# A decoder block with retention, gated DeltaNet and PEER experts on one core: norms held as columns, a search list of 112 sums, and another dealing of the expert turns

## The reference, cut to what matters

```python
h = rmsnorm(x, ln1_w); proj = h @ w_in        # 14 blocks of 256 columns, and 8 columns a, b
# retention, 4 heads (q, k of 64, v of 128), chunks of 128 tokens
# gated DeltaNet, 4 heads of 128: q, k, v = silu(causal conv of 4 taps)
q_g = q_g * rsqrt(sum(q_g * q_g) + eps)        # per token and head
k_g = k_g * rsqrt(sum(k_g * k_g) + eps)
# kkt = (beta k) k^T * lmask, triangular solve, o = S^T q / sqrt(128), S updated per chunk
x = x + concat(y_r, y_g) @ w_out
h2 = rmsnorm(x, ln2_w)
q = (h2 @ wq)                                  # 8 heads x 2 halves x 128
s = q . sub_keys                               # 128 scores per head and half
s1, i1 = top_k(s[first half], 16); s2, i2 = top_k(s[second half], 16)
cand = s1[:, None] + s2[None, :]               # 256 sums per head
best, pos = top_k(cand, 16)                    # 16 experts per head, 128 per token
gate = softmax(best)
x = x + sum_k gate_k * gelu(u[id_k] . h2) * v[id_k]
y = rmsnorm(x, lnf_w)
```

## Time and profile before

| | |
|---|---|
| median of 3 runs | 3363.88 us (3355.34 to 3367.5) |
| the profiled execution | 3368.8 us, its span 3367.0 us |
| mean granted TensorE clock | 0.858 |
| busy: PE, DVE, ACT, POOL | 2454.9, 2158.9, 1171.7, 1177.1 us |
| bytes moved by DMA | 1266.28 MB, mean 376 GB/s |
| gathers (queue 0), weights and others (queue 1) | 1073.81 MB, 183.84 MB |

### The profile page before, as it was taken

How to read it: one execution, slowest core, us unless ns; L and a number is a source line. 1 busy time by engine, 2 the same in 40 slices (tenths; PEclk the granted TensorE clock), 3 DMA queues, 4 the chain that set the end, 5 groups by cost and what they waited for, 6 DMA issues and landing times.

```text
span 3367.0 us, 35982 instructions
## 1 busy us (share of the span) xinstructions
PE 2454.9 (73%) x12432; PEld 1395.4 (41%) x12432; DVE 2158.9 (64%) x5332; ACT 1171.7 (35%) x3379; POOL 1177.1 (35%) x1030
## 2 busy tenths in 40 slices
PE   7579878646889968755879968855788757865555
PEld 6478445313457534411456624611355324521111
DVE  0525684788556785588746677487846677477444
ACT  1121533334432543234324343335233253333222
POOL 0002342433433334343423334343433324344442
PEclk9788999877899988867999979977889879987777
DMA  6047999998999999998999989999899989999998
GB/s 243 12 163 282 415 368 392 387 421 360 400 415 395 421 369 405 382 421 361 406 419 382 421 367 393 400 421 414 360 409 420 422 367 411 419 394 422 422 421 344
DMA packets 176438, 1266.28 MB, mean 376 GB/s; under 512 B 20096, under 2 KB 20096, under 8 KB 23808
## 3 DMA queue, kind: packets, MB, share of 16 engines
q0 software_dynamic: 147456, 1073.81, 77.8%
q1 hardware_dynamic: 26928, 183.84, 13.6%
q10 hardware_dynamic: 1872, 6.33, 0.5%
HBM read 1259.71 MB, written 4.19 MB: 375 GB/s over the span
## 4 chain that ended last, share of the span: by engine, by line
PE 38%; DMA 27%; DVE 23%; ACT 8%; issue 3%; POOL 1%; another core or an unknown queue 0%; ACTq 0%; DVEq 0%; SPq 0%; POOLq 0%
DMA uv<-uv_tab,ids 18%; PE y_ps L374 13%; DVE uv L865 10%; PE bank L430 10%; DMA wbuf<-w 10%; PE bank L422 8%; PE bank L437 3%; DVE area L916 2%; ACT diag L633 2%; DVE area L954 2%; POOL uv L352 1%; PE bank L603 1%; DVE area L1122 1%; ACT gelu L627 1%; PE bank L398 1%
## 5 line engine op out<-in xcount | busy, mean ns | idle before, releaser
L352 POOL DMA_INDIRECT uv<-uv_tab,ids x1024 | 1176.6, 1149 | 2161.9 <-PE y_ps L374 1713.9
L374 PE MATMUL y_ps<-uv,diag 128*64 128x512 f32 x4096 | 1235.8, 737 | 671.9 <-ACT diag L633 627.6
L865 DVE CUSTOM_DVE_ANT_0 uv<-uv,h 128x1024 f32<-128x1024 f32 x1024 | 1227.4, 1222 | 600.1 <-DMA uv<-uv_tab,ids 589.0
L374 PEld LDWEIGHTS y_ps<-uv,diag 128*64 128x64 f32 x4096 | 294.1, 159 | 1390.4 <-ACT diag L633 891.1
L627 ACT ACTIVATE gelu<-dots 128x2 f32<-128x2 f32 x512 | 103.6, 202 | 1307.3 <-DVE dots L865 1294.6
L430 PE MATMUL bank<-actT,wbuf 128*128 128x128 f32 x3008 | 383.4, 290 | 82.8 <-DMA wbuf<-w 77.6
L430 PEld LDWEIGHTS bank<-actT,wbuf 128*128 128x128 f32 x3008 | 368.2, 204 | 137.1 <-issue 75.8
L633 ACT ACTIVATE diag<-gated,gelu 128x64 f32<-128x64 f32 x1024 | 300.8, 340 | 59.6 <-ACT gelu L627 1.6
L422 PE MATMUL bank<-wbuf,actT 128*128 128x256 f32 x1152 | 279.8, 399 | 25.6 <-DMA wbuf<-w 24.2
L623 ACT ACTIVATE gated<-smalls,gate 128x64 f32<-128x64 f32 x1024 | 293.9, 335 | 7.8 <-DVE acc L879 7.8
L422 PEld LDWEIGHTS bank<-wbuf,actT 128*128 128x128 f32 x1152 | 223.7, 199 | 110.0 <-issue 62.9
(11 more groups left out here) (190 smaller groups left out, 1805.3 us busy)
## 6 DMA issues: line engine op xcount, KB each, us to landing
wbuf<-w SPq DMA_DIRECT2D x166, 1024.0 KB
uv<-uv_tab,ids POOLq DMA_INDIRECT x1024
acc<-x SPq DMA_DIRECT2D x8, 512.0 KB
y<-acc ACTq DMA_DIRECT2D x8, 512.0 KB
rowbuf<-x SPq DMA_DIRECT2D x5, 512.0 KB, 12.2
actT_ahead<-x SPq DMA_DIRECT2D x3, 512.0 KB, 14.9
keys_sb<-keysT ACTq DMA_DIRECT2D x1, 1024.0 KB, 7.6
tab<-tables SPq DMA_DIRECT2D x1, 960.0 KB, 5.3
```

The lines of the kernel that those rows point to most:

```text
L352: nc.gpsimd.indirect_dma_start(out=uv[i % RING][:, :, :].rearrange("p z d -> p (z d)"), out_offset=None, in_=uv_tab, in_offset=bass.Indire ...
L374: done = mm(y_ps[z][64 * j:64 * j + 64, :], diag[:, i % DIAGS, :], uv[i % RING][:, 1, 512 * z:512 * z + 512], start=(s % PAIRS == 0), stop ...
L865: V.tensor_tensor_reduce(out=u, in0=u, in1=h2[n % 2][:, j, :], scale=1.0, scalar=0.0, op0=ALU.mult, op1=ALU.add, accum_out=dots[:, i % DOT ...
```

## The change

The norms stay columns: TensorE multiplies each 128x128 block of squares by one column of ones (8 products into one bank, `ss`), ScalarE takes the root of 128x4 twice, VectorE a reciprocal of 128x8. The factor of k goes into beta (`TT`), into the scales of `kbe` and `kst` and into `cmask`; the factor of q goes into the square of `gdn_out` and into the factor of the last norm. q and k themselves are no longer scaled, so their transposes and q k^T don't wait for it. The convolution takes k first, then q, then v. The search list has 112 of the 256 sums: those of the first 4 with all 16, and of the other 12 with the first 4; positions are turned back by a few small instructions. `picked` is multiplied for four heads at once. `PIECES` has 34 entries, `window` depends on the kind of the next chunk, and `DIAGS` is 6.

```diff
-DIAGS = 8
+DIAGS = 6
+CANDS = 4 * TOPK + (TOPK - 4) * 4
...
-    uses += own(("gc", "gc_in", 1, 0), ("gc_row", "E", 1, 0), ("beta_row", "kbT", 1, 0),
-                ("ssq", "norm_in", 2, 0), ("ssk", "norm_in", 2, 1),
-                ("kT", "kst", 1, 0), ("vT", "vb", 1, 0), ("kk", "NT", 1, 0), ("qk", "attn", 1, 0),
+    uses += own(("gc", "gc_in", 1, 0), ("gc_row", "E", 1, 0), ("ss", "norm_in", 1, 0),
+                ("kT", "kst", 1, 0), ("qk", "attn", 1, 0), ("beta_row", "kbT", 1, 0),
+                ("vT", "vb", 1, 0), ("kk", "NT", 1, 0),
...
-PIECES = ([5, 7, 4.5, 3, 3, 7, 5, 6, 5] + [5, 4, 3, 4, 6, 4, 5, 4, 3.5, 4, 3, 4] + [3, 3, 7, 4] + [4, 4, 4, 4] + [4, 5]
-          + [4, 4, 4, 4])
+PIECES = ([2, 2.3, 1.7, 1, 1.6, 1.2, 2, 1.5]
+          + [1.2, 0.8, 0.7, 0.8, 1.3, 0.8, 1.2, 0.8, 0.7, 0.8, 0.5, 0.8] + [0.6, 0.8, 1.4, 0.6]
+          + [1.15, 1.15, 1.15, 1.15] + [0.8, 0.8] + [1.15, 1.15, 1.15, 1.15])
+WINDOW = {"first": (20, 10), "second": (15, 5), "alone": (17, 7), None: (15, 5)}
...
-    return (-14, 14) if n == 0 else (PAIRS * n - 20, PAIRS * n + 10)
+    if n == 0:
+        return -14, 14
+    before, after = WINDOW[KIND[n + 1] if n + 1 < NCH else None]
+    return PAIRS * n - before, PAIRS * n + after
...
@@ tensor, mix @@
                 all_rows(n, "gc_row", T[:, :, :])
+                pe.wait_ge(*event("sq", n))
+                b = take(n, "ss")
+                for i in range(2 * H):
+                    last = mm(b[:, i:i + 1], norms[:, i, :], ones[:, 0:1], start=True, stop=True)
+                given(last)
+                turn()
+                transposes(n, "kT", lambda i: conv[:, 4 + i, :], 4)
+                by_head(n, "qk", conv[:, 4:8, :], conv[:, 0:4, :])
+                turn()
+                pe.wait_ge(*event("beta_k", n))
                 all_rows(n, "beta_row", TT[:, :, :])
-                turn()
-                turn()
-                pe.wait_ge(*event("sq", n))
-                all_rows(n, "ssq", norms[:, 0:4, :])
-                all_rows(n, "ssk", norms[:, 4:8, :])
-                turn()
-                turn()
-                pe.wait_ge(*event("normed", n))
-                transposes(n, "kT", lambda i: conv[:, 4 + i, :], 4)
+                pe.wait_ge(*event("silu_conv", n, 2))
                 transposes(n, "vT", lambda i: conv[:, 8 + i, :], 4)
+                turn()
...
-                by_head(n, "qk", conv[:, 4:8, :], conv[:, 0:4, :])
...
@@ scalar, mix @@
+                conv_silu(2, 2)
+                b = filled(act, "ss", c)
+                A(st[:, root][:, 0:H], b[:, 0:H], ACT.Sqrt, bias=eps_col[:, 1:2], scale=float(DV))
+                A(st[:, root][:, H:2 * H], b[:, H:2 * H], ACT.Sqrt, bias=eps_col[:, 0:1]).then_inc(S["norm_in"], 1)
                 turn()
...
-                put("norm_in", "ssq", norms[:, 0:4, :], c, ACT.Sqrt, bias=eps_col[:, 0:1])
-                put("norm_in", "ssk", norms[:, 4:8, :], c, ACT.Sqrt, bias=eps_col[:, 0:1])
...
@@ vector, mix @@
+                dve.wait_ge(*event("norm_in", n))
+                link(V.reciprocal(st[:, 64:72], st[:, root]))
+                link(V.tensor_tensor(st[:, 52:56], st[:, 24:28], st[:, of_k], ALU.mult))
+                V.tensor_tensor(TT[:, :, :], each_head(ident), by_head(st[:, 52:56]), ALU.mult).then_inc(S["beta_k"], 1)
                 dve.wait_ge(*event("exp_diff", n))
-                V.tensor_tensor(st[:, 36:40], st[:, 36:40], st[:, 24:28], ALU.mult)
-                link(V.tensor_tensor(cmask[:, :, :], cmask[:, :, :], each_head(causal), ALU.mult))
-                turn()
-
-                dve.wait_ge(*event("norm_in", n, 1))
-                link(V.reciprocal(norms[:, :, :], norms[:, :, :]))
-                turn()
-                V.scalar_tensor_tensor(conv[:, 0:4, :].rearrange("p h t -> p (h t)"),
-                                       conv[:, 0:4, :].rearrange("p h t -> p (h t)"), float(DV) ** -0.5,
-                                       norms[:, 0:4, :].rearrange("p h t -> p (h t)"), ALU.mult, ALU.mult)
-                V.tensor_tensor(conv[:, 4:8, :], conv[:, 4:8, :], norms[:, 4:8, :], ALU.mult).then_inc(S["normed"], 1)
-                dve.wait_ge(*event("normed", n))
+                V.tensor_tensor(st[:, 36:40], st[:, 36:40], st[:, 52:56], ALU.mult)
+                V.tensor_tensor(st[:, 40:44], st[:, 40:44], st[:, of_k], ALU.mult)
+                for h in range(H):
+                    last = V.scalar_tensor_tensor(cmask[:, h, :], cmask[:, h, :], st[:, of_k][:, h:h + 1], causal,
+                                                  ALU.mult, ALU.mult)
+                link(last)
+                turn()
...
+                link(V.tensor_tensor(st[:, 28:32], st[:, 28:32], st[:, of_q], ALU.mult))
...
@@ vector, route @@
-                    for h in some:
+                    heads4 = slice(4 * g, 4 * g + 4)
+                    pairs = top_v[:, halves, :].rearrange("p (h z) k -> p h z k", z=2)
+                    for a0, a1, width, at_ in ((0, 4, TOPK, 0), (4, TOPK, 4, 4 * TOPK)):
                         last = V.tensor_tensor(
-                            cand[:, h, :].rearrange("p (a b) -> p a b", b=TOPK),
-                            top_v[:, 2 * h, :].unsqueeze(2).broadcast_to([P, TOPK, TOPK]),
-                            top_v[:, 2 * h + 1, :].unsqueeze(1).broadcast_to([P, TOPK, TOPK]), ALU.add)
+                            cand[:, heads4, at_:at_ + (a1 - a0) * width].rearrange("p h (a b) -> p h a b", b=width),
+                            pairs[:, :, 0, a0:a1].unsqueeze(3).broadcast_to([P, 4, a1 - a0, width]),
+                            pairs[:, :, 1, 0:width].unsqueeze(2).broadcast_to([P, 4, a1 - a0, width]), ALU.add)
...
-                    top16(some, lambda t: cand[:, t, :], lambda t: best[:, t, :],
+                    top16(some, lambda t: cand[:, t, 0:CANDS], lambda t: best[:, t, :],
...
-                    link(V.tensor_scalar(pos2[:, 1, mine], pos[:, mine], TOPK - 1, None, ALU.bitwise_and))
+                    V.tensor_scalar(pos2[:, 1, mine], pos[:, mine], 2, None, ALU.logical_shift_right)
+                    link(V.tensor_copy(flat_pos[:, mine], pos[:, mine]))
                     link(V.tensor_copy(pos_f[:, :, mine], pos2[:, :, mine]))
+                    link(V.scalar_tensor_tensor(pos_f[:, 0, mine], pos_f[:, 1, mine], -12.0, pos_f[:, 0, mine],
+                                                ALU.add, ALU.max))
+                    link(V.tensor_scalar(pos_f[:, 1, mine], pos_f[:, 0, mine], 4.0, 48.0, ALU.mult, ALU.add))
+                    link(V.scalar_tensor_tensor(pos_f[:, 1, mine], pos_f[:, 0, mine], 16.0, pos_f[:, 1, mine],
+                                                ALU.mult, ALU.min))
+                    link(V.tensor_tensor(pos_f[:, 1, mine], flat_pos[:, mine], pos_f[:, 1, mine], ALU.subtract))
...
-                        for h in some:
-                            one_head = picked[:, TOPK * h:TOPK * h + TOPK, :]
-                            last = V.tensor_tensor(one_head, one_head, top_if[:, 2 * h + z, :].unsqueeze(1)
-                                                   .broadcast_to([P, TOPK, TOPK]), ALU.mult)
-                        link(last)
+                        by_slot = pk.rearrange("p (h s) k -> p h s k", s=TOPK)
+                        index = top_if[:, halves, :].rearrange("p (h z) k -> p h z k", z=2)[:, :, z, :]
+                        link(V.tensor_tensor(by_slot, by_slot, index.unsqueeze(2).broadcast_to([P, 4, TOPK, TOPK]), ALU.mult))
```

More of the change, by code:

```diff
@@ L187, in build @@
         exp_a = sb("exp_a", [H])
-        eps_col = sb("eps_col", [1])
+        eps_col = sb("eps_col", [2])
         w_ab_sb = sb("w_ab_sb", [KT, 2 * H])
@@ L232, in build @@
         picked = scores.rearrange("p a (b t) -> p (a b) t", t=TOPK)
-        st = sb("st", [64])
+        st = sb("st", [80])
+        of_q, of_k, root = slice(64, 68), slice(68, 72), slice(72, 80)
         bn = sb("bn", [H, 6])
@@ L240, in build @@
         top_i, pos2, pos = piece(5, 16, U32), row(6, U32), row(7, U32)[:, 0, :]
+        flat_pos = row(7)[:, 1, :]
         iota_f = sb("iota_f", [TOPK])
@@ L258, in build @@
             "ss1": 1, "sqrt1": 1, "rstd1": 1, "x_norm": 1, "rot": 1, "ret_qd": 1, "ret_out_ready": 1, "sqrt_ret": 1,
-            "ret_mixed": 1, "conv_done": 3, "silu_conv": 3, "sq": 1, "normed": 1, "sp_in": 1, "exp_ab": 1,
+            "ret_mixed": 1, "conv_done": 3, "silu_conv": 3, "sq": 1, "beta_k": 1, "sp_in": 1, "exp_ab": 1,
             "ln_ab": 1, "beta_g": 1, "diff": 1, "exp_diff": 1, "small_exp": 1, "kst_scale": 1, "qd": 1,
@@ L487, in mix @@
                 all_rows(n, "gc_row", T[:, :, :])
+                pe.wait_ge(*event("sq", n))
[8 more added lines that the diff above has]
+                pe.wait_ge(*event("beta_k", n))
                 all_rows(n, "beta_row", TT[:, :, :])
+                pe.wait_ge(*event("silu_conv", n, 2))
+                transposes(n, "vT", lambda i: conv[:, 8 + i, :], 4)
                 turn()
-                turn()
```

(34 more changed lines are left out.)

2 lines of the change are left out of this document (removed).

## The result

The changed kernel takes 3264.5 us (median of 4 runs, 3261.8 to 3270.4) against 3365.7 (4 runs, 3355.3 to 3373.0): ratio 0.9704, 95% interval 0.9674 to 0.9734, so some 100 us faster. Forecast were 3314 and a range of 3255 to 3348: the direction is right and the time lies inside the range, but the forecast had half the gain. The profiled execution has a span of 3260.0 us, 107 less than before.

The account below looks back on a forecast made before the run. DMA at 421.5 GB/s bounds the kernel; only 363 us short of work can be won. Start-up -10, mix starts -58, weight blocks +15, VectorE +8, some 5 freed search time: -50, giving 3314 us (3255 to 3348).

Parts of the forecast that it names:

- The holes: Whole span: time in which the DMA engines were short of work, 363 us, the only time that can be won.
- Start-up, -10: Before any gather: norms as columns bring NT from 115.65 to 105.6 us, gain 10 us, bounds 6 and 12.
- Mix starts, -58: Seven mix starts, 79 us lost: less VectorE work and more steps leave 3 us each; gain 58, bounds 37 and 72.
- the ring: Mix starts: VectorE has 17 us too much work, 12 are lost, so the ring of 9 covers 5.
- Weight blocks at the window starts, +15: Windows 1, 3, 5, 7: three steps instead of four in 28 us, 10 us lost each; 15 more, bounds 0 and 20.
- The two double projections: Windows opening with double projections: dips of 5 us each, 10 in all; windows 2 and 4 keep theirs.
- VectorE in windows of 20 steps, +8: Four short windows: VectorE needs 99 us against 110 but idles 13, so 2 late each; 8 more, bounds 0 and 40.
- Levels, 0: Level pieces shrink from 11.0 to 9.5 steps, 5 us more; output projection's weight blocks 5 less; together 0, bounds 15.
- The first rival: Nearly all losses go if the ring covers weight blocks and short windows: 3242 to 3278 us; chance 0.25.
- the 13 us without a step: Short windows: argued against the losses going; TensorE's 13 us without a step is in the program's order and stays.
- the second: Rival: mix-start losses only move into the search window; 3335 us, with start-up alone 3354; chance 0.13.
- the third: Rival: slower, half a search does not fit into 10 steps and `routed` comes 12 us late; 3376 us; chance 0.06.

Follow-up runs that it names:

- e9: Changed kernel with a step between any two weight blocks in 20-step windows and 42-step mixes' levels dealt as in 39; 3236.5 us, 0.9609.
- e12: Changed kernel with a step between any two weight blocks in 20-step windows and twelve equal level pieces in all mixes; 3235.8 us, 0.9610.
- e2: Kernel before (old norms, full search) with only the new windows and pieces, old proportions kept in the first nine; 3303.4 us, 0.9823.
- e10: Kernel before with DIAGS 6 in place of 8 and nothing else; 3368.3 us, 1.0002.
- e3: Kernel before with the short search list alone (112 sums, one product by index for four heads); 3366.1 us, 1.0002.
- e1: Changed kernel with the old deal: windows of 30 steps and old pieces, new proportions in the first eight; 3291.9 us, 0.9779.
- e8: Kernel before with a constant written in place of the reciprocal of the norms, norms left out of the result; 3322.6 us, 0.9865.
- e7: Changed kernel where the two 42-step mixes deal 39 as the others and give 3 more steps to the first eight pieces; 3256.3 us, 0.9662.
- e6: Changed kernel with a step between any two weight blocks of q2 and q3 in the four 20-step windows; 3249.8 us, 0.9641.
- e5: Changed kernel with the windows of before (30 steps each, mix 34) and the new pieces; 3333.7 us, 0.9899.
- e11: Changed kernel with the windows of before and new pieces, but equal shares with the same sum for the twelve level pieces; 3267.4 us, 0.9704.

## Why the prediction was right, and where its sizes were off

**The bound.** The ceiling of 421.5 GB/s held: in no kernel run here does any of the 40 slices of the span show more than 422. The holes, 363 us before, are 256 in the changed kernel and 230 and 229 in e9 and e12.

**Start-up, -10.** From the first instruction behind the ScalarE wait to NT it was 86.12 to 115.65 before and is 83.04 to 101.70 now: 10.9 us less. The other 3 us are ahead of the change. The first dots come at 280.8 to 284.7 us in three kernels with the old norms and the old list (before, e2, e10) and at 266.1 to 276.8 in eight that start as the changed one does, so 14 is one pair of a gain of about 12.

```profile
83.04 0.17 DVE L941 TENSOR_SCALAR st<-st 128x4 f32<-128x4 f32 x1 [41.38 <-ACT st L750]
...
90.81 3.57 PE L500 MATMUL bank<-tab,area 128*128 128x1 f32 x16 [3.77 <-ACT area L756]
...
95.93 1.28 ACT L764 ACT_TABLE_LOAD   x1
97.22 0.63 ACT L764 ACTIVATE decayT<-decayT 128x512 f32<-128x512 f32 x1
...
101.70 0.68 DVE L980 TENSOR_TENSOR arena<-bank,decayT 128x512 f32<-128x512 f32 x1
```

The 16 small products took 3.57 us (3.4 forecast). The function follows its table load at once (95.93 + 1.28 = 97.21), so the drain that the Trainium skill adds (ScalarE: Activation LUTs, What ACT_TABLE_LOAD costs) is not seen here, and the forecast by rows was the right one. That the search list is worth nothing at start-up also held: VectorE waits 14.2 us for the gates' exp after as it did before, and with the list alone (e3) the first dots come at 288.0 us.

**Mix starts, -58: the step that was mis-sized.** The mechanism was the right one (e1, e2, e8), the remainder was not: I left 3 us in each for latencies and single pieces that go over, and 0 to 1.3 us stayed: -80 by the sums over packets. The margin and the ring take up more than I allowed. The margin itself was misread: by `PIECES` the eight pieces get 13.7 steps of 39, not 14.9, which counts the first piece of the levels too. So the sum should have read 63.8 us of VectorE (55.4 and 3.6 steps at 2.35) against 68.2 of gathers, a margin of 4. That the losses went even so makes the 3 us kept in each the worse guess. The same count holds for e2: 67 and 8.5 us of VectorE against 68.2 are an excess of 7, not 4, so 2 us should have stayed in each, and 3.4 did; in e1, with an excess of 5, 2.5 stayed. The ring's cover of 5 us is no sharp edge.

**Weight blocks at the window starts, +15: wrong in sign.** I had counted one step less in the same 28 us and forecast a loss of 10 us per window; it is 3 to 7, before 5 to 8, together 4 us less. The 4 us are no gain that is shown: the same four window starts lack 25 to 30 us in four kernels with the old deal and the old order of the norms (before, e3, e8, e10), 21 in the changed kernel and 28 in e7. The sign that I had named, 200 to 250 GB/s over 20 us, was not seen either: the lowest 20 us of these four windows are at 290, 307, 339 and 357. That two blocks without a step between them cost is shown by e6; that they would cost more than before was not so. What differs ahead of them, the wider places of the eight earlier blocks (1.18 steps in place of 0.89), may let them begin with a fuller ring; no run here isolates that. The Trainium skill (DMA: Bandwidth & Descriptors, Queues, rings and completion order) says that each DMA engine takes turns between its queues, packet by packet; by that the prediction had estimated 5 us for a block. In the changed kernel the page of the profile has a median of 9.3 us from issue to landing, so the row was the better guide to the load, if not to its effect:

```profile
wbuf<-w SPq DMA_DIRECT2D x166, 1024.0 KB, 9.3
```

The two double projections, whose dips I had kept, also lost less, by 11 us: they lack 2 to 7 us in all seven kernels with the new windows, 7 to 16 in those with the old.

**VectorE in windows of 20 steps, +8: wrong.** The work was about right (102.8 us busy in the row above, which has the dots of 20 steps; 99 were forecast), the time was not: that stretch took 127 us, not 110. In it pass 51.2 MB, 44.8 of gathers (20 steps are 41.9) and 5.8 of weights; that is 122 us of transfers, and 5 us were lost at its start. So there was more room than I gave it: steps 58 to 74 lack 2.5 us in all seven chunks together.

**Levels, 0: right in the sum, by luck.** +1 us, made of 18 us more in the two mixes of 42 steps and 17 less in the others. My argument, 1.5 steps fewer, was wrong twice. By `PIECES` the twelve level pieces go from 11.0 steps to 10.7 of 39, not to 9.5; and 9 whole steps in the levels of chunk 1 lose nothing while 12 in those of chunk 6 lose 12 us. What counts here is that no turn lets two steps through beside one that lets none (e5, e11, e7), as long as the steps are not too few (8 in chunk 1 of e5 and e11).

So the forecast of -50 became -107 by the spans: 22 us from the mix starts, 19 from the weight blocks, 11 from the double projections, 8 from VectorE's windows and 4 from start-up, less 5 of freed search time in the long windows that didn't show and 2 of small parts. These are differences of one pair of profiled executions, and the terms under 10 us are no finer than the noise. The first rival (the losses all but go) came nearer than the forecast; the objection to it, the 13 us without a step, was real but small. Nothing shows the second and the third: the windows did not lose what the mix starts won, and GpSimd waits for `routed` once only, 263.1 us at the start.

## What to carry to other kernels

Where a transfer queue is the bound and the engines follow a written order, add up for each stretch what the busiest engine has to do against the transfer time dealt to it: the excess, less the ring's cover, is about the loss (within 3 us on the mean of the seven mix starts in each kernel here), and less work or more time cure it equally, not twice. Fractional shares of a stream that moves in whole steps should be checked as the whole numbers they become, above all where two engines pass a result back and forth at each turn: 2 0 where 1 1 was meant cost some 4 to 6 us a time, an estimate: 12 us for three in a mix of 42 steps, some 11 more in each mix of 34 steps for the two in e5 than in e11. Work taken off an engine that has room in that stretch (the search list here) brings nothing until the stretch is made short.
